# One kernel, two blocks of a network: another order for the first transfers (rows and two token tiles, then the first weight alone, then the rest)

## What is computed

```python
def rms_norm(x, g):
    xf = x.astype(jnp.float32)
    y = xf * lax.rsqrt(jnp.mean(xf * xf, axis=-1, keepdims=True) + EPS)
    return (y * g.astype(jnp.float32)).astype(x.dtype)

n = rms_norm(h, g_mix[i])
z = n @ w_in[i] + b_in[i]
q, k, v, u, bg, cg, ga, gc = jnp.split(z, SPLITS, axis=-1)
```

## Time and profile before

| | |
|---|---|
| median of 3 runs | 1785.29 us (1783.28 to 1789.4) |
| the profiled execution: its own time | 1784.8 us |
| the profiled execution: span in the trace | 1782.9 us |
| TensorE busy in the span | 1714.0 us (96%) |
| VectorE busy | 866.3 us (49%) |
| ScalarE busy | 372.6 us (21%) |
| GpSimd busy | 209.6 us (12%) |

### The profile page before, as it was taken

The page is one execution under the profiler, slowest core; times in us unless marked ns, Lnnn a source line. Parts: engine busy times, 40 slices in busy tenths (PEclk is TensorE's granted clock), DMA queues, the critical chain, the costliest instruction groups (busy, mean ns, idle before and its releaser), DMA issues.

```text
span 1782.9 us, 19612 instructions
## 1 busy us (share of the span) xinstructions
PE 1714.0 (96%) x7538; PEld 999.7 (56%) x7538; DVE 866.3 (49%) x1505; ACT 372.6 (21%) x659; POOL 209.6 (12%) x280
## 2 busy tenths in 40 slices
PE   6999999997899999999989999999899999999999
PEld 3887876674433333333334464768655544667664
DVE  3756743445423233232324447666755554557553
ACT  1122220001100000000003112320244325344330
POOL 1234310001000000000001100011154400000000
PEclk9999999998999999999999999999999999999989
DMA  7322131255699999999991113132300021112101
GB/s 278 112 70 108 48 107 47 101 212 198 252 400 427 427 427 427 425 428 428 426 407 61 60 59 118 48 120 101 113 36 1 13 80 75 48 48 95 48 1 48
DMA packets 27873, 308.61 MB, mean 173 GB/s; under 512 B 4415, under 2 KB 4703, under 8 KB 10368
## 3 DMA queue, kind: packets, MB, share of 16 engines
q1 hardware_dynamic: 21312, 289.21, 39.8%
q0 software_dynamic: 6464, 18.10, 3.0%
HBM read 306.57 MB, written 4.19 MB: 174 GB/s over the span
## 4 chain that ended last, share of the span: by engine, by line
PE 87%; DVE 7%; DMA 2%; issue 1%; ACT 1%; POOL 0%; SPq 0%; DVEq 0%; ACTq 0%
PE ps L411 83%; PE ps L414 5%; DVE arena L1168 4%; DMA wring<-in_w 2%; DVE arena L1179 1%; ACT arena L2296 1%; DMA H<-in_x 1%; DVE wring L1168 0%; DVE arena L1195 0%; DVE small L1183 0%; DVE arena L1264 0%; POOL small L2708 0%; DVE HT L1195 0%; ACT L2296 0%; DVE H L1168 0%
## 5 line engine op out<-in xcount | busy, mean ns | idle before, releaser
L411 PE MATMUL ps<-arena 128*64 128x512 f32 (+13 forms) x2384 | 535.1, 401 | 9.2 <-DVE arena L1173 3.8
L411 PE MATMUL ps<-wring,arena 128*64 128x512 f32 (+2 forms) x1136 | 399.4, 583 | 6.8 <-DMA wring<-in_w 4.3
L411 PEld LDWEIGHTS ps<-arena 128*64 128x64 f32 (+3 forms) x2384 | 244.8, 154 | 232.9 <-issue 217.0
L411 PE MATMUL ps<-wring,HT 128*128 128x512 f32 (+1 forms) x1040 | 363.0, 502 | 4.3 <-ACT HT L2296 1.9
L1168 DVE TENSOR_TENSOR arena<-ps,arena 128x512 f32<-128x512 f32 (+1 forms) x197 | 134.9, 685 | 478.0 <-PE ps L411 314.6
L411 PEld LDWEIGHTS ps<-wring,HT 128*128 128x128 f32 x1040 | 194.3, 191 | 143.5 <-issue 128.7
L2296 ACT ACTIVATE arena<-ps 128x512 f32<-128x512 f32 (+3 forms) x163 | 88.5, 543 | 641.4 <-PE ps L414 332.5
L411 PEld LDWEIGHTS ps<-wring,arena 128*64 128x64 f32 (+1 forms) x1136 | 148.8, 155 | 128.6 <-issue 125.2
L411 PE MATMUL ps<-HT,wring 128*128 128x512 f32 (+2 forms) x528 | 194.9, 534 | 2.2 <-DVE arena L1195 2.2
L411 PE MATMUL ps<-wring 128*128 128x256 f32 x816 | 188.3, 385 | 3.5 <-DVE arena L1168 3.5
L1168 DVE TENSOR_TENSOR H<-ps,H 128x512 f32<-128x512 f32 x182 | 126.0, 692 | 98.1 <-PE ps L411 95.5
(11 more groups left out here) (106 smaller groups left out, 990.4 us busy)
## 6 DMA issues: line engine op xcount, KB each, us to landing
wring<-in_w SPq DMA_DIRECT2D x48, 2048.0 KB, 20.2
wring<-in_dense SPq DMA_DIRECT2D x39, 2048.0 KB, 8.2
arena<-in_w SPq DMA_DIRECT2D x36, 2048.0 KB, 17.6
HT<-in_w SPq DMA_DIRECT2D x12, 2048.0 KB, 16.8
arena<-in_rows POOLq DMA_DIRECT2D x33, 256.0 KB, 5.1
H<-in_x SPq DMA_DIRECT2D x4, 512.0 KB, 9.4
arena<-in_relb POOLq DMA_DIRECT2D x8, 256.0 KB, 8.3
n_scratch<-arena POOLq DMA_DIRECT2D x4, 512.0 KB, 3.3
```

The costliest lines, as they stand in the source:

```text
L411: return nc.tensor.matmul(o, l, r, start=start, stop=stop, skip_group_check=True)
```

## The change

SP now issues tile 0, `ident`, `gmix0`, `gmix1` and tile 1, waits until `gmix1` has landed, issues `w_q`, waits until `w_q` has landed, and only then issues tiles 2 and 3, `w_k`, `pcl`, `con` and `w_v`. POOL no longer issues its rows 2 and 3 first: it takes the roots of tiles 0 and 1, then issues these two rows, then takes the roots of tiles 2 and 3. No computation is added or removed, and the programs of TensorE, VectorE and ScalarE stay as they are.

```diff
@@ POOL
+            g.wait_ge(S("ident"), 16)
+            for i in range(2):
+                norm_root(i)
             row(2, 3)
-            g.wait_ge(S("ident"), 16)
-            for i in range(4):
+            for i in (2, 3):
                 norm_root(i)
             for h in range(4):
                 bias(h)
@@ SP
             for n in range(2):
                 sp.dma_start(rowbuf[n], T["rows"][ROWS["g_mix"] + n, :].partition_broadcast(128)).then_inc(S(f"gmix{n}"), 16)
-            for i in range(1, 4):
-                sp.dma_start(H[:, i, :], xv[:, i, :]).then_inc(S(f"x{i}"), 16)
+            sp.dma_start(H[:, 1, :], xv[:, 1, :]).then_inc(S("x1"), 16)
@@ SP, behind the definition of load
+            sp.wait_ge(S("gmix1"), 16)
             load("w_q")
+            sp.wait_ge(S("w0"), 16)
+            for i in (2, 3):
+                sp.dma_start(H[:, i, :], xv[:, i, :]).then_inc(S(f"x{i}"), 16)
             load("w_k")
             sp.dma_start(pcl[:, :], T["pcl"]).then_inc(S("pcl"), 16)
             sp.dma_start(con[:, 130:], T["con"][:, 130:]).then_inc(S("con"), 16)
```

## The result

The changed kernel takes 1788.38 us (median of 20 runs, 1782.46 to 1793.9); the kernel before, now with 20 runs too, 1783.22 us (1778.42 to 1790.3). The ratio is 1.0026, 95% interval 1.0015 to 1.0036: 4.6 us slower, between 2.7 and 6.4 (the two medians themselves differ by 5.2). The forecast was 6.2 us slower and 1791.5 us.

The account below looks back on a forecast made before the run. TensorE, busy for 96% of the span, was taken to bound the kernel. Tile 2's later start, 5.7 us, plus 0.5 for the clock made 6.2, so 1785.3 became 1791.5 us; range 1787.2 to 1795.6.

Parts of the forecast that it names:

- The change puts three transfers in series and tile 2 at their end: At the start: `gmix1`, `w_q`, then tile 2 land one after another; PE starts on tile 2 5.7 us later.
- Rows 2 and 3 cost the front 2.2 us: GpSimd's queue at the start: without these rows first, `gmix1` lands at 7.6 instead of 9.83.
- `w_q` from issue to landing, 8.6 us: SP's queue: `w_q`, issued at about 7.7 behind `gmix1`, lands at 16.3; bounds 13.2 and 18.7.
- The second way, 16.6: Second estimate of `w_q`'s landing: 19.0 before, less 2.4 us for tiles 2 and 3, nothing off for the rows.
- Tile 2 lands 3.4 behind its issue: SP's queue after `w_q`'s landing: tile 2 starts at 16.35, takes 3.4 like tile 0, lands at 19.75.
- The clock, +0.5: TensorE at the first projection: longer idling delays the clock's rise, costing 0.5 us; bounds -0.7 and +1.8.
- Pays its whole latency again.: Tile 2, formerly in a queue that never ran dry, now starts after a full landing and takes 3.4 us.
- PE's order excludes an earlier projection: PE transposes tiles 0, 1 and 2 before waiting for `w_q`, so a projection 3.3 us earlier is impossible.
- No cover is used up: Tile 3, `w_k`, `con`, bias tables and rows come later but before their use; costed at nothing.
- A shift runs through to the end: Later loads are released by PE, so a shift of PE's start reaches the end of the kernel unchanged.
- the sign that the prediction had named: Wrong if the distance from first projection to end of span changes by more than 2 us.
- rival 1: A loss too small to tell: `w_q` lands before 15.5, PE on tile 2 before about 22.7; 1790.0 or 1789.4; chance 0.33.

Follow-up runs that it names:

- SP part alone: Changed kernel with GpSimd's old order (rows 2 and 3 first), SP's new order and both waits kept; ratio 1.0042 to the kernel before.
- GpSimd part alone: Kernel before with only GpSimd's rows 2 and 3 moved behind the root of tile 1; ratio 0.999 to the kernel before.
- the run with those rows later: Changed kernel without SP's wait for `w_q`, and GpSimd's rows 2 and 3 behind all four roots; ratio 1.0011 to the kernel before.
- the run with no wait: Changed kernel without both SP waits, and TensorE projecting tile 0 before transposing tile 2; ratio 0.9979 to the kernel before.

## Why the prediction came out as it did

- *The change puts three transfers in series and tile 2 at their end.* Right. The chain names them in that order, and PE is idle for 8.3 us.
- *Rows 2 and 3 cost the front 2.2 us.* Right: `gmix1` landed at 7.64, predicted 7.6. The SP part alone, which keeps those rows in front, has it at 9.47, and the mark 2.5 us later. So the rows cost `gmix1` 1.8 us with SP's new order; with its old order they cost 2.3 (9.82 before, 7.54 with the GpSimd part alone).
- *`w_q` from issue to landing, 8.6 us.* Too long by 0.9: 7.68, the value of a weight with nearly empty queues in the earlier trace rows. I had let the two rows hold it up, and the run with those rows later, where it took 7.98 against 8.05, shows that they don't. The second way, 16.6, had the same fault: it put their 2.2 us back in full.
- *Tile 2 lands 3.4 behind its issue.* 3.81, too short by 0.4, with GpSimd's rows beside it (3.37 without them in the SP part alone); the way through the norm 3.76 against 3.78. Together with `w_q`, PE starts on tile 2 5.1 us late instead of 5.7.
- *The clock, +0.5.* 0.0: the first 32 records took 14.73 us against 14.70. The bounds were right to be kept: the two projections took up to 15.89 in the other kernels.
- *"Pays its whole latency again."* Right for this kernel: 3.81 us from a landed `w_q` to a landed tile, against 1.3 in the queue without waits. As a statement on the one wait it would be wrong: taken out alone, it gives back 0.3 us, since the tile then shares the engines with GpSimd's rows, and moving these away from it gives 1.6. It takes both waits out to get the tile back by 4.4. The prediction costed the changed kernel as it stands and needed none of this, so its sum could be right without it.
- *PE's order excludes an earlier projection.* Right. With that order changed the same transfers win 2.0 us at the mark, instead of losing 5.2; the GpSimd part alone wins 2.2 without it.
- *No cover is used up.* Right: `w_k`, `con` and the tables made nobody wait.
- *A shift runs through to the end.* Supported by all eleven comparisons within their intervals, and not by the sign that the prediction had named, the distance from the first projection to the end: it changed by 7.2 us between the two profiled executions, through less time at the low clock and shorter pauses of PE later in the kernel, where executions differ anyway.
- *The size.* The forecast stood 1.0 us above the shift at the mark (6.2 against 5.2), and that is the 0.9, -0.4 and 0.5 above: the tile's error took back part of the weight's, which is luck. The loss of 4.6 us, and the 5.2 of the medians, lie under the 5.4 at which the forecast's bracket began, so they fall on the side of rival 1, a loss too small to tell. Its landmarks were met or nearly so: `w_q` landed before 15.5, and PE started on tile 2 at 22.93 where it had named 22.7. The interval of the ratio excludes that there was no loss, and does not exclude 5.4, so the result doesn't decide between the two.
- In the prediction, the estimate from the Trainium skill's page "DMA: Bandwidth & Descriptors" gave the weight 6.8 us from issue to landing. The runs show 7.7 to 8.1 on SP's queue wherever it was issued behind `gmix1`. That estimate's time, 1789.0, lies nearer to the measured 1788.38 than the forecast does, but by luck: its start on tile 2, 21.5, is 1.4 us too early, and the kernel before had come out 2.1 us lower.

## What to carry to other kernels

A transfer is early enough only relative to the order in which the engine that uses it takes its inputs. Before moving one ahead, read that order: here tile 2, the third input in TensorE's program, was put behind the weight, the fourth. Split a change that moves several queues: its halves had opposite signs here, -2.2 and +7.6 us. And when several waits stand in series, take out all of them too, and not only one at a time: here one gave back at most 0.4 us at tile 2, and both gave 4.4. Where a gain is a few microseconds in 1783, read it at a mark in the trace that lies just behind the change, then check it against the timed ratio.

## What the runs showed that I had not expected

- A wait on a 2 MB landing, taken out, moved the landing of the next 0.5 MB from 19.17 to 18.86 only, and with the wait ahead of it gone as well to 14.78. Two rows of 256 KB from GpSimd, issued at 11 us, went with a tile 1.6 us later behind the weight, and the weight itself no later that can be seen; in the run with no wait, issued at 10.69, most of them moved only behind the tile, and it landed 1.3 us behind the weight.
- The first projections ran at the lower level of TensorE's clock for very different times. The first 16 records took 8.87, 9.13, 9.15 and 10.16 us in four kernels, where 16 records at 2.4 GHz take 7.03. The pause of PE just ahead of them doesn't order them: it was 0.81 us ahead of the 9.13, 2.10 ahead of the 9.15 and 1.70 ahead of the 10.16. What sets the time at the lower level stays open. The granted clock printed for these stretches is 1.00, and only the durations show it.
- Fourteen transposes that nobody needs, run ahead of the real ones, raised TensorE's clock for these (1.16 instead of 1.97 us for eight). Pauses of 1.6 to 1.8 us were followed by a fall at 14 us, with a mean granted clock of 0.58 and 0.56 in the next two windows of 2 us.
